# Attention of a two-layer hybrid backbone step: from one head at a time to pairs of heads, with bias and exponential in PSUM

## The reference, cut to what matters

```python
def context_attention(q, k, v):            # 128 queries, 128 keys
    ...
        s = jnp.einsum('bhqd,bhkd->bhqk', q_blk, k).astype(jnp.float32)
        pr = jax.nn.softmax(s, axis=-1).astype(v.dtype)
        return jnp.einsum('bhqk,bhkd->bhqd', pr, v)

def neighbourhood_attention(q, k, v, k_ctx, v_ctx, rpb_l):
    ...
    s_win = jnp.einsum('bhrqd,bhrkwd->bhrqkw', qg, kg).astype(jnp.float32) + bias.astype(jnp.float32)
    s_win = jnp.where(col_mask[:, None, :], s_win, NEG_INF).reshape(bsz, heads, rows, GRID_W, kr * GRID_W)
    s_ctx = jnp.einsum('bhrqd,bhld->bhrql', qg, k_ctx).astype(jnp.float32)
    pr = jax.nn.softmax(jnp.concatenate([s_win, s_ctx], axis=-1), axis=-1).astype(v.dtype)
    ...
    o = (jnp.einsum('bhrqkw,bhrkwd->bhrqd', p_win, vg)
         + jnp.einsum('bhrql,bhld->bhrqd', p_ctx, v_ctx))
```

## Time and profile before

| what | value |
|---|---|
| median of 3 runs | 2135.04 us (2134.25 to 2135.24) |
| span of the profiled execution, first to last instruction | 2131.6 us |
| PE busy over the span | 1916.8 us, 90% |
| DVE busy | 909.3 us, 43% |
| ACT busy | 675.0 us, 32% |
| mean granted clock of TensorE | 0.911 of full speed |

### The profile page before, as it was taken

How to read it: one execution, slowest core, us unless ns; L and a number is a source line. 1 busy time by engine, 2 the same in 40 slices (tenths; PEclk the granted TensorE clock), 3 DMA queues, 4 the chain that set the end, 5 groups by cost and what they waited for, 6 DMA issues and landing times.

```text
span 2131.6 us, 20882 instructions
## 1 busy us (share of the span) xinstructions
PE 1916.8 (90%) x7660; PEld 1289.0 (60%) x7661; DVE 909.3 (43%) x1352; ACT 675.0 (32%) x1026; POOL 109.5 (5%) x93
## 2 busy tenths in 40 slices
PE   6999898899996798999779898989999898999793
PEld 2444444788886796554656565656666566666562
DVE  0303602433335724442545555555555544333454
ACT  1103211433324222221234444444444443221342
POOL 2111110000000500000010000000000000000001
PEclk9999998999998897557679999999999999999897
DMA  9565659333334423001559999999999997544792
GB/s 298 188 214 182 198 203 358 121 119 119 99 119 93 125 80 99 1 1 59 178 173 303 324 325 314 333 315 313 307 326 301 322 299 261 178 148 159 235 297 110
DMA packets 359072, 436.78 MB, mean 205 GB/s; under 512 B 32332, under 2 KB 311528, under 8 KB 358968
## 3 DMA queue, kind: packets, MB, share of 16 engines
q1 hardware_dynamic: 334160, 397.44, 57.4%
q10 hardware_dynamic: 20456, 25.21, 3.4%
q0 software_dynamic: 4352, 12.88, 1.7%
HBM read 417.57 MB, written 17.93 MB: 204 GB/s over the span
## 4 chain that ended last, share of the span: by engine, by line
PE 81%; DVE 9%; issue 5%; ACTq 2%; ACT 2%; DMA 1%; DVEq 0%; POOL 0%; POOLq 0%
PE ps L1601 33%; PE ps L1618 15%; PE ps L1525 7%; PE ps L1566 5%; PE ps L1498 4%; PE ps L1629 4%; PE ps L1668 3%; PE ps L1731 3%; PE ps L1707 2%; DVE split L1219 2%; PE ps L1580 2%; PE ps L1680 2%; ACTq L821 2%; DVE ring_split L1283 1%; DVE extra_split L1283 1%
## 5 line engine op out<-in xcount | busy, mean ns | idle before, releaser
L1601 PE MATMUL ps<-split,hi_x 128*128 128x512 f32 (+1 forms) x2304 | 693.4, 386 | 25.0 <-issue 20.2
L1219 DVE TENSOR_TENSOR split<-ring,split 128x1024 fp32r<-128x1024 f32 (+1 forms) x432 | 469.1, 1131 | 103.3 <-ACT split L829 101.4
L1601 PEld LDWEIGHTS ps<-split,hi_x 128*128 128x128 f32 x2304 | 419.8, 193 | 110.6 <-issue 33.2
L1601 PE MATMUL ps<-split,lo_x 128*128 128x512 f32 (+1 forms) x1152 | 438.8, 381 | 0.0
L829 ACT ACTIVATE split<-ring 128x1024 fp32r<-128x1024 f32 (+1 forms) x432 | 389.3, 977 | 52.7 <-issue 35.2
L1618 PE MATMUL ps<-ring,work 128*128 128x512 f32 x792 | 357.9, 593 | 3.7 <-DVE work L1252 3.7
L857 ACT ACTIVATE work<-ps 128x256 f32<-128x256 f32 (+1 forms) x144 | 52.8, 367 | 691.8 <-PE ps L1601 691.7
L1246 DVE TENSOR_TENSOR work<-work,ps 128x256 f32<-128x256 f32 (+1 forms) x144 | 57.4, 399 | 479.1 <-ACT work L857 432.1
L1601 PEld LDWEIGHTS ps<-split,lo_x 128*128 128x128 f32 x1152 | 220.8, 192 | 42.1
L1618 PEld LDWEIGHTS ps<-ring,work 128*128 128x128 f32 x792 | 147.9, 189 | 150.6 <-issue 142.8
L1525 PE MATMUL ps<-ring,cond 128*2 128x256 f32 x576 | 128.0, 383 | 9.6 <-DMA ring<-in_w_mod_dram 9.6
(11 more groups left out here) (219 smaller groups left out, 1575.7 us busy)
## 6 DMA issues: line engine op xcount, KB each, us to landing
ring<-in_moe_w_gate_dram SPq DMA_DIRECT2D x80, 1024.0 KB, 7.4
ring<-in_moe_w_up_dram SPq DMA_DIRECT2D x80, 1024.0 KB, 9.9
ring<-in_moe_w_down_dram SPq DMA_DIRECT2D x80, 1024.0 KB, 5.1
ring<-in_w_mod_dram SPq DMA_DIRECT2D x36, 1024.0 KB, 7.4
mod_extra<-in_w_mod_dram SPq DMA_DIRECT2D x12, 1024.0 KB, 6.9
ring<-in_w_qkv_dram SPq DMA_DIRECT2D x6, 2048.0 KB, 8.9
ring<-in_w_in_dram SPq DMA_DIRECT2D x5, 2048.0 KB, 10.3
ring<-in_ffn_w_gate_dram SPq DMA_DIRECT2D x10, 1024.0 KB, 7.7
```

Source lines behind the costliest of these rows:

```text
L1219: dve.tensor_tensor(low, raw, high.bitcast(F32), ALU.subtract).then_inc(lo_ok, 1)
L1601: ins = pe.matmul(ps[:, 0, 0:2 * w], xt(c_), split[:, j % 2, part, c_, 0:2 * w], start=(c_ == 0 and n == 0), stop=(c_ == KC - 1 and n == 2))
```

## The change

Attention runs over 24 pairs of heads instead of 48 units. In scores, each product of a head is cut into two of half the columns (192 latent, 64 context), and the two heads, which lie on the two halves of the partitions, take turns: head 0 part 0, head 1 part 0, head 0 part 1, head 1 part 1, into a bank for each head. DVE adds the bias of both heads in one instruction in place in PSUM, and one reduction gives the negated maximum of both heads; `s_buf` is gone. ACT's exponential reads PSUM. The reciprocal is one for two heads; the multiplication stays one for each head. Transposes write one bank for each head (4 and 5), without a second buffer. Value products take turns between the heads for each block of keys, and write the two halves of the partitions of bank 6 or 7 (four pairs to a bank); the output is copied in six pieces of 512 columns. Scores now wait for the exponentials of two pairs before (`p_ok`). The probability buffers and one of the two buffers for transposed probabilities move to other places in SBUF.

```diff
         v_tok = at(o + 2 * KC * W + D, TILES, D)
         o += 2 * KC * W + TILES * D
         vc = at(o + D, D)
-        s_buf = mod_extra[:, 0:768].rearrange("p (a b) -> p a b", a=2)
-        p_buf = mod_extra[:, 768:1920].rearrange("p (a b) -> p a b", a=3)
-        pt_buf = at(o + 2 * D, 2, 384)
+        p_buf = [mod_extra[:, 0:768], mod_extra[:, 768:1536], xn[:, D:D + 768]]
+        pt_buf = [xn[:, D + 768:D + 1536], at(o + 2 * D, 768)]
         kc_tok = at(o + 2 * D, D)
         k_out = xn[:, 0:D]
         sums = at(o + 3 * D, TILES, HEADS)
-        mx = at(o + 3 * D + 48, 2, 1)
-        nmx = at(o + 3 * D + 50, 2, 1)
+        nmx = at(o + 3 * D + 48, 2, 2)
         assert o + 3 * D + 52 <= WORK
...
         PB = 6
-        units = [(t, h) for t in (1, 2, 0) for h in range(HEADS)]
+        pairs = [(t, c_) for t in (1, 2, 0) for c_ in range(KC)]
         def reverse(v):
...
             act.wait_ge(ctx_t, 1)
             act.activation(kc_t[:, 4:8, :], ps[:, 7, :].rearrange("p (a b) -> p a b", a=4), ACT.Copy).then_inc(ctx_ok, 1)
+
             def prob_turned(u):
-                n = 384 if units[u][0] else P
-                act.wait_ge(pt_ps, u + 1)
+                n = 384 if pairs[u][0] else P
                 if u >= 2:
                     act.wait_ge(pv, u - 1)
-                act.activation(pt_buf[:, u % 2, 0:n], ps[:, 2 + u % 2, 0:n], ACT.Copy).then_inc(pt_ok, 1)
-
-            for u, (t, h) in enumerate(units):
+                for k in range(2):
+                    act.wait_ge(pt_ps, 2 * u + k + 1)
+                    act.activation(pt_buf[u % 2][:, k * 384:k * 384 + n], ps[:, 4 + k, 0:n], ACT.Copy).then_inc(pt_ok, 1)
+
+            for u, (t, c_) in enumerate(pairs):
                 n = 384 if t else P
                 act.wait_ge(max_ok, u + 1)
                 if u >= 3:
-                    act.wait_ge(pt_ps, u - 2)
-                act.activation(p_buf[:, u % 3, 0:n], s_buf[:, u % 2, 0:n], ACT.Exp, bias=nmx[:, u % 2, :],
-                               accum_out=sums[:, t, h:h + 1]).then_inc(p_ok, 1)
+                    act.wait_ge(pt_ps, 2 * (u - 2))
+                for k in range(2):
+                    act.activation(p_buf[u % 3][:, k * 384:k * 384 + n], ps[:, 2 * (u % 2) + k, 0:n], ACT.Exp,
+                                   bias=nmx[:, u % 2, k:k + 1],
+                                   accum_out=sums[:, t, 2 * c_ + k:2 * c_ + k + 1]).then_inc(p_ok, 1)
                 if u >= 2:
                     prob_turned(u - 2)
-            prob_turned(len(units) - 2)
-            prob_turned(len(units) - 1)
+            prob_turned(len(pairs) - 2)
+            prob_turned(len(pairs) - 1)
             norm(3)
...
             def divide(u):
-                t, h = units[u]
+                t, c_ = pairs[u]
                 n = 384 if t else P
-                dve.wait_ge(p_ok, u + 1)
-                ordered(dve.reciprocal(sums[:, t, h:h + 1], sums[:, t, h:h + 1]))
-                dve.tensor_scalar(p_buf[:, u % 3, 0:n], p_buf[:, u % 3, 0:n], sums[:, t, h:h + 1], None,
-                                  ALU.mult).then_inc(pn_ok, 1)
-
-            def output_in(ti, tt):
-
-                dve.wait_ge(pv, HEADS * (ti + 1))
-                src = ps[:, 4 + 2 * (ti % 2):6 + 2 * (ti % 2), :].rearrange("p a (c q) -> p (a c) q", q=P)
-                dve.tensor_copy(hn_t[:, :, TOK[tt]:TOK[tt] + P], src[:, :, ::-1] if tt else src).then_inc(o_ok, 1)
+                dve.wait_ge(p_ok, 2 * u + 2)
+                both = sums[:, t, 2 * c_:2 * c_ + 2]
+                ordered(dve.reciprocal(both, both))
+                for k in range(2):
+                    prob = p_buf[u % 3][:, k * 384:k * 384 + n]
+                    ins = dve.tensor_scalar(prob, prob, sums[:, t, 2 * c_ + k:2 * c_ + k + 1], None, ALU.mult)
+                ins.then_inc(pn_ok, 1)
+
+            def output_in(e):
+
+                tt, hf = (1, 2, 0)[e // 2], e % 2
+                dve.wait_ge(pv, 4 * (e + 1))
+                src = ps[:, 6 + hf, :].rearrange("p (c q) -> p c q", q=P)
+                dve.tensor_copy(hn_t[:, 4 * hf:4 * hf + 4, TOK[tt]:TOK[tt] + P],
+                                src[:, :, ::-1] if tt else src).then_inc(o_ok, 1)
             dve.wait_ge(bias_ok, 1)
-            for u, (t, h) in enumerate(units):
+            n_biased = 0
+            for u, (t, c_) in enumerate(pairs):
                 n = 384 if t else P
+                b0 = 2 * (u % 2)
                 dve.wait_ge(sc_ps, u + 1)
-                if u >= 2:
-                    dve.wait_ge(p_ok, u - 1)
                 if t:
-                    j0 = 6 * h + 2 - 2 * (t - 1)
-                    dve.tensor_tensor(s_buf[:, u % 2, 0:256].rearrange("p (a b) -> p a b", a=4),
-                                      ps[:, u % 2, 0:256].rearrange("p (a b) -> p a b", a=4),
-                                      bias[:, j0:j0 + 4, :], ALU.add).then_inc(s_ok, 1)
-                    dve.tensor_copy(s_buf[:, u % 2, 256:384], ps[:, u % 2, 256:384]).then_inc(s_ok, 1)
-                else:
-                    dve.sem_inc(s_ok, 1)
-                    dve.tensor_copy(s_buf[:, u % 2, 0:P], ps[:, u % 2, 0:P]).then_inc(s_ok, 1)
-                dve.wait_ge(s_ok, 2 * u + 2)
-                ordered(dve.tensor_reduce(mx[:, u % 2, :], s_buf[:, u % 2, 0:n], AX_X, ALU.max))
-                dve.tensor_scalar(nmx[:, u % 2, :], mx[:, u % 2, :], -1.0, None, ALU.mult).then_inc(max_ok, 1)
+                    j0 = 2 - 2 * (t - 1)
+                    near = bias[:, 12 * c_:12 * c_ + 12, :].rearrange("p (k a) b -> p k (a b)", k=2)
+                    dve.tensor_tensor(ps[:, b0:b0 + 2, 0:256], ps[:, b0:b0 + 2, 0:256],
+                                      near[:, :, j0 * GRID_W:(j0 + 4) * GRID_W], ALU.add).then_inc(s_ok, 1)
+                    n_biased += 1
+                    dve.wait_ge(s_ok, n_biased)
+                dve.tensor_reduce(nmx[:, u % 2, :], ps[:, b0:b0 + 2, 0:n], AX_X, ALU.max, negate=True).then_inc(max_ok, 1)
                 if u:
                     divide(u - 1)
-
-                for ti, tt in enumerate((1, 2)):
-                    if u == HEADS * (ti + 1) + 4:
-                        output_in(ti, tt)
-            divide(len(units) - 1)
-            output_in(2, 0)
+                if u >= 7 and u % 4 == 3:
+                    output_in(u // 4 - 1)
+            divide(len(pairs) - 1)
+            output_in(5)
             dve.wait_ge(st_kv, 32)
             residual(2, lambda t, hf: 3 * hf + t)
...
             pe.wait_ge(v_ok, 3)
             pe.wait_ge(s_vc, 16)
-            n_units = len(units)
-            for u in range(n_units + 3):
-                if u < n_units:
-                    t, h = units[u]
-                    r, ci = 64 * (h % 2), h // 2
+            n_pairs = len(pairs)
+            for u in range(n_pairs + 3):
+                if u < n_pairs:
+                    t, c_ = pairs[u]
                     if u >= 2:
-                        pe.wait_ge(s_ok, 2 * (u - 1))
-                    q = q_t[r:r + 64, ci, TOK[t]:TOK[t] + P]
-                    if t:
-                        ins = pe.matmul(ps[:, u % 2, 0:384], q, kk_t[r:r + 64, ci, S0:W + P], start=True, stop=True)
-                    else:
-                        ins = pe.matmul(ps[:, u % 2, 0:P], q, kk_t[r:r + 64, ci, 0:P], start=True, stop=True)
+                        pe.wait_ge(p_ok, 2 * (u - 1))
+                    first, half = (S0, 192) if t else (0, 64)
+                    for part in range(2):
+                        lo = part * half
+                        for k in range(2):
+                            r = slice(HD * k, HD * k + HD)
+                            ins = pe.matmul(ps[:, 2 * (u % 2) + k, lo:lo + half], q_t[r, c_, TOK[t]:TOK[t] + P],
+                                            kk_t[r, c_, first + lo:first + lo + half], start=True, stop=True)
                     ins.then_inc(sc_ps, 1)
-                if 2 <= u <= n_units + 1:
+                if 2 <= u <= n_pairs + 1:
                     w_ = u - 2
-                    tp = units[w_][0]
+                    tp = pairs[w_][0]
                     pe.wait_ge(pn_ok, w_ + 1)
-                    if w_ >= 2:
-                        pe.wait_ge(pt_ok, w_ - 1)
-                    for b in range(3 if tp else 1):
-                        ins = turn(ps[:, 2 + w_ % 2, b * P:(b + 1) * P], p_buf[:, w_ % 3, b * P:(b + 1) * P])
-                    ins.then_inc(pt_ps, 1)
+                    for k in range(2):
+                        if w_:
+                            pe.wait_ge(pt_ok, 2 * w_ - 1 + k)
+                        for b in range(3 if tp else 1):
+                            ins = turn(ps[:, 4 + k, b * P:(b + 1) * P],
+                                       p_buf[w_ % 3][:, k * 384 + b * P:k * 384 + (b + 1) * P])
+                        ins.then_inc(pt_ps, 1)
                 if u >= 3:
                     w_ = u - 3
-                    tp, hp = units[w_]
-                    ti = w_ // HEADS
```

(20 more changed lines are left out.)

## The result

The changed kernel takes 2012.51 us (median of 4 runs, 2010.36 to 2016.45), the kernel before 2134.64 beside it: 0.9433 of the time, 95% interval 0.9416 to 0.945. The profiled execution has a span of 2014.7 us, 116.9 less than before.

The account below looks back on a forecast made before the run. Attention was taken as bound by PE at half clock. At high clock with overlapping halves, its 154.3 us fall to 77: span 2131.6 - 77 = 2054.6, with 3.4 around it 2058 us; range 2046 to 2097.

Parts of the forecast that it names:

- that copy: Attention's last output copy, at 977.5 us, where the output product starts; all later work was said to wait for it.
- The stage: Attention, 154.3 us before; forecast at 77 us with high clock and overlapping halves, a gain of 77; chance 0.50.
- Clock: TensorE's clock in attention: from 0.50 (1.2 GHz) to 1.00 (2.4 GHz) within the first pairs, holding through the latent tiles.
- the three rises: Clock rises outside attention: during modulation products, after 24 transposes, 5.6 us into the output product; each after unpaused full-row PE work.
- Overlap: Two heads' records run at once on PE's halves: eight score records take 5 steps, twelve value records 7.
- rival 4: Slower: every change of half drains PE for 0.19 us, adding 30 to 145.2 at low clock: 2156 us; chance 0.04.
- No row shows two halves side by side in time: Claim about the profile before, which left halves in turn and full overlap as the bounds for PE in attention.
- Latent pair: Two heads on a latent tile: 3.17 us a pair at 2.4 GHz with overlap, half a 6.33 us round of waits.
- Context pair: Two heads on the context tile: 1.8 us a pair at 2.4 GHz, eight pairs, score records held up by weight loads.
- First four pairs: Start of attention: 6.3 us for three pairs still at 1.2 GHz, on top of full latent rounds of 3.17 each.
- The output product: Product behind attention: it may find the clock high, which saves half of 5.6 us.
- 3.4 above: Median of the runs over the profiled span, 2135.0 against 2131.6, added to the forecast span of 2054.6 for 2058.

Follow-up runs that it names:

- pad203: Changed kernel plus 203 tiny early DVE writes, putting DVE's loop over the expert rounds back at instruction 832: 2048.28 us (0.9593 of before).
- pad53before: Kernel before plus 53 tiny early DVE writes, so that DVE's loop over the expert rounds starts at instruction 885: 2103.63 us (0.9859).
- single: Changed kernel with PE's list by heads again (scores, transposes, values of head 0, then head 1), pairs kept on DVE and ACT: 2103.45 us (0.9864).
- filledbefore: Kernel before with the new keys' transfer issued on GpSimd and 26 idle transposes in PE's pauses before the stage and around the first exponential: 2076.62 us (0.9736).
- inturn: Changed kernel with all of head 0's records, then all of head 1's, in scores and in value products: 2014.63 us (0.9446).
- poolbefore: Kernel before with the new keys' transfer issued on GpSimd instead of ACT: 2130.67 us (0.9985).

## Why the prediction was wrong

**The step that failed** is "All that comes later hangs on that copy, so a microsecond taken from the stage is one taken from the end". It holds for the data (+1.4 us up to the rounds, -0.1 at the end), but the change also takes 203 instructions out of DVE's list ahead of a loop, and that loop's code is fetched again in the rounds or not by its place: pad203 and pad53before move 31 to 36 us with it (31 in the rounds of either trace), in either direction and with either attention. Of the 39.9 us between the forecast span (2054.6) and the measured one, 30.3 are this. The sign stood in the trace of before: waits of 9 us with no releaser at the start of five rounds, and 55 instruction fetches. The count of instructions stood in the diff.

**The stage** was right in mechanism and mis-sized, 77 forecast and 65.7 measured:
- Clock: it rises within the first pairs and holds, as forecast. The reason, that half-row products in short groups keep it down, is half right: that order doesn't lift it (single), but holds it (filledbefore). Of the three rises that the forecast leans on, shows two: the windows of the modulation products both stand at 1.00.
- Overlap: it comes, and a change of half costs nothing (rival 4 falls). But it takes 4 and 6 steps, not 5 and 7: two heads' value group lasts 0.88, one head's 0.87 (filledbefore), and two heads' scores 0.92 against 0.91. The Trainium skill ("TensorEngine Tiling (Array Packing)", Key Properties) says that tiles load and multiply in parallel; these pairs of rows agree. "No row shows two halves side by side in time" was wrong: the first row has four records of two heads in 1.65 us, where a single head's two take 1.58.
- Latent pair: 3.02 us from the scores' starts at 838.26 and 874.49 over 12 pairs; 3.17 forecast. Maximum 0.957 and bias 0.699 came as priced (0.95, 0.69), copies at 0.493 (0.47), exponentials at 0.576 (0.61), and the groups on PE shorter.
- Context pair: 1.5 us (1.8), since the two halves' loads run side by side too (eight score records in 0.66 us, where eight loads one behind the other, at half of the 0.216 in the earlier trace rows, make 0.86), and the clock stayed. From its first scores to the product 18.0 us (20.4 by the forecast's terms).
- First four pairs, 826.73 to 838.26: 11.5 us, where 4 x 3.17 + 6.3 = 19.0 had been summed. This is the largest error inside the stage, 7.5 of 11.3 us: at the start a pair is scores alone, and I charged whole rounds and the low clock on top.

**The rest.** The output product found the clock high and gave 2.8 us, as supposed. The last 5.6 us of the miss are the runs: the median lies 2.2 us under the profiled span, where 3.4 above was taken.

Of the 116.9 us between the spans, then, 30.3 go to the place of DVE's loop, 53.9 to the clock alone (154.3 to 100.4 us, filledbefore), 34.7 to pairs (100.4 to 65.7), and -2.0 to the start, the product and the routing. The shares hang together: in the changed kernel the order by pairs is also what brings the clock back, and the 34.7 hold the clock of the context units too, which filledbefore loses (25.5 us at 0.55). What in the order of records lifts it is not settled: single differs from the changed kernel both in overlap and in the length of the groups, and inturn kept both.

## What to carry to other kernels

A change in an engine's instruction count moves every loop behind it: look for waits that nothing releases and that come back round after round, and for the page's instruction fetches, and try a few idle instructions ahead of the loop before crediting or blaming the change. Where TensorE stands at half clock under full load, look at the pauses in front of the stage first; some idle transposes there may give most of what a rewrite gives. And read the first, unpipelined group of a stage: it shows what overlaps.

## What the hardware showed that was not expected

- A loop of 330 DVE instructions costs 6.1 us more a round at one place than at three others; fetches of 8 KB go from 18 to 55. PE's loop seems to have such places too: two kernels with 52 and 53 fetches of 16 KB have a gap of 7.4 us that two others, with 49, lack.
- TensorE's clock depends on its past: the same records in the same order, with PE busy for 97% of the time in either case, stand at 0.50 for 155 us or at 1.00 for 75 us, by whether PE had paused in front of them (3.5 us in the kernel before; 1.32, 0.78 and 0.78 us in poolbefore).
- Two heads on the two halves of the rows cost one head's time (0.92 against 0.91 us), and scores do so in turn as well as alternated; six records to a head, in turn, overlap in part (1.14 against 0.88).
